# Sixteen places for the weight spreads of an expert loop, own sum banks for its second token tile, and later reads

## What is computed

```
q = h @ wq                                   # 8 heads, two halves of 128
sc = einsum(q, subkeys)                      # 128 keys for each half
vals, ids = top_k(sc, 16)                    # per half
top, pos = top_k(all 16 x 16 sums, 16)       # 16 experts per head, 128 per token
idx = the expert numbers (of 16384), g = softmax(top)
for the 128 experts k of a token:
    a   = dot(peer_u[idx_k], h)              # a row of 1024
    wgt = g_k * gelu(a)
    out += wgt * peer_v[idx_k]               # a row of 1024
x = x + gate2 * out
```

## Time and profile before

| what | us |
|---|---|
| median of 3 runs (1365.33 to 1369.11) | 1368.21 |
| the profiled execution, its own time | 1367.95 |
| its span, first to last instruction | 1366.2 |
| busy: PE / DVE / POOL / ACT | 1222.2 / 866.4 / 521.8 / 425.4 |
| expert loop, first gather to last sum | 174.7 to 870.4 |

### The profile page before, as it was taken

How to read it: one execution, slowest core, us unless ns; L and a number is a source line. 1 busy time by engine, 2 the same in 40 slices (tenths; PEclk the granted TensorE clock), 3 DMA queues, 4 the chain that set the end, 5 groups by cost and what they waited for, 6 DMA issues and landing times.

```text
span 1366.2 us, 14256 instructions
## 1 busy us (share of the span) xinstructions
PE 1222.2 (89%) x4539; PEld 642.2 (47%) x4539; DVE 866.4 (63%) x1726; ACT 425.4 (31%) x1126; POOL 521.8 (38%) x578
## 2 busy tenths in 40 slices
PE   7999979999877877877898777899999999999997
PEld 2676545565322222323443222564444445999443
DVE  2446478575575766777667578568997443677335
ACT  2212244333443343443434434322115111222000
POOL 1000057665777776777777777001111000000000
PEclk9999999999999999999999999999999999999999
DMA  9797599999999999999999999363333344354440
GB/s 346 294 328 278 171 334 398 406 406 404 405 409 410 409 409 409 392 409 409 409 409 407 408 406 404 145 246 123 124 123 124 107 157 166 140 183 146 169 181 31
DMA packets 130794, 397.32 MB, mean 291 GB/s; under 512 B 10380, under 2 KB 11788, under 8 KB 130463
## 3 DMA queue, kind: packets, MB, share of 16 engines
q0 software_dynamic: 74448, 271.09, 50.3%
q1 hardware_dynamic: 54404, 120.14, 24.4%
q10 hardware_dynamic: 1868, 5.18, 1.0%
HBM read 395.32 MB, written 1.05 MB: 290 GB/s over the span
## 4 chain that ended last, share of the span: by engine, by line
PE 46%; DMA 22%; POOL 12%; DVE 10%; issue 5%; DVEq 3%; ACT 1%; POOLq 0%; ACTq 0%
PE psum L673 18%; DMA gathered<-in_peer_u_dram,expert_idx 16%; PE psum L1270 6%; PE psum L1309 6%; POOL gathered L582 6%; POOL gathered L596 6%; PE psum L985 6%; DMA gathered<-in_peer_v_dram,expert_idx 3%; DVE work L1771 3%; DMA weight_ring<-in_w_in_dram 2%; DVE gathered L2116 2%; DVE work L2405 2%; PE psum L781 2%; PE psum L700 1%; PE psum L755 1%
## 5 line engine op out<-in xcount | busy, mean ns | idle before, releaser
L985 PE MATMUL psum<-gathered,modr 128*128 128x512 f32 x1024 | 500.1, 618 | 115.1 <-DMA gathered<-in_peer_v_dram,expert_idx 96.9
L2116 DVE CUSTOM_DVE_ANT_0 gathered<-gathered,psum 128x1024 f32<-128x1024 f32 x256 | 312.2, 1220 | 181.4 <-DMA gathered<-in_peer_u_dram,expert_idx 180.0
L985 PEld LDWEIGHTS psum<-gathered,modr 128*128 128x128 f32 x1024 | 180.0, 192 | 412.9 <-DMA gathered<-in_peer_v_dram,expert_idx 245.9
L582 POOL DMA_INDIRECT gathered<-in_peer_u_dram,expert_idx x256 | 249.0, 972 | 265.1 <-DVE expert_idx L1779 167.4
L596 POOL DMA_INDIRECT gathered<-in_peer_v_dram,expert_idx x256 | 243.8, 952 | 92.5 <-issue 70.8
L673 PE MATMUL psum<-weight_ring,featT 128*128 128x512 f32 x384 | 172.2, 603 | 1.7 <-ACT featT L1361 1.7
L1524 ACT ACTIVATE gel<-dots 128x1 f32<-128x1 f32 x256 | 51.6, 201 | 285.6 <-DVEq L2118 285.4
L1771 DVE TENSOR_TENSOR work<-work 128x1088 f32<-128x1088 f32 (+4 forms) x107 | 99.9, 951 | 26.8 <-ACT work L1624 18.7
L673 PEld LDWEIGHTS psum<-weight_ring,featT 128*128 128x128 f32 x384 | 71.7, 191 | 92.2 <-issue 90.0
L673 PE MATMUL psum<-featT,weight_ring 128*128 128x128 f32 (+2 forms) x768 | 107.6, 296 | 3.6 <-ACT featT L1361 1.5
L673 PEld LDWEIGHTS psum<-featT,weight_ring 128*128 128x128 f32 x768 | 100.6, 191 | 19.2 <-issue 11.5
(11 more groups left out here) (365 smaller groups left out, 1370.0 us busy)
## 6 DMA issues: line engine op xcount, KB each, us to landing
weight_ring<-in_w_in_dram SPq DMA_DIRECT2D x13, 2048.0 KB, 9.1
weight_ring<-in_ada_w_dram SPq DMA_DIRECT2D x10, 2048.0 KB, 17.5
weight_ring<-in_w_up_dram SPq DMA_DIRECT2D x8, 2048.0 KB, 8.3
weight_ring<-in_w_down_dram SPq DMA_DIRECT2D x8, 2048.0 KB, 7.7
weight_ring<-in_peer_wq_dram SPq DMA_DIRECT2D x3, 2048.0 KB, 12.7
gathered<-in_ada_w_dram SPq DMA_DIRECT2D x2, 2048.0 KB, 14.6
gathered<-in_w_in_dram SPq DMA_DIRECT2D x2, 2048.0 KB, 13.4
gathered<-in_peer_u_dram,expert_idx POOLq DMA_INDIRECT x256, 11.0
```

The lines of the kernel that those rows point to most:

```text
L582: pool.indirect_dma_start(u_rows[:, slot, :], None, T["peer_u"], bass.IndirectOffsetOnAxis(ap=expert_idx[:, r % 2, k:k + 1], axis=0),).the ...
L985: mm = pe.matmul(psum[:, SUM_BANK + half, :], diag[:, e % 8, :], v_rows[:, slot, 512 * half:512 * (half + 1)], start=(e % EXPERTS == 0), s ...
L2116: dve.tensor_tensor_reduce(u_rows[:, slot, :], u_rows[:, slot, :], h2_rows[t], 1.0, 0.0, ALU.mult, ALU.add, dots[:, col:col + 1])
```

## The change

- **Places for spreads.** `diag` gets eight more places, in `vec`. `rotate` gives each of the 256 experts the least recently used place: eight up to expert 75 of tile 0, sixteen from expert 76 on. ACT waits for the expert that last had the place.
- **Sum banks.** `sum_bank` gives tile 0 banks 2 and 3 and tile 1 banks 6 and 7. `u0` and `q20` move to banks 2 and 3. PE's wait for `sum_read` moves from tile 1's first expert to the first `u0` product, expert 58. DVE reads tile 0's sums after expert 14.
- **Reads and their places.** ACT reads tile 0's second-block products (and `meta`, `h0`, ln0) six experts behind PE. `u0` and `q20` stand every fourth expert, from 58 and from 76; ln0 every fourth from 84 in tile 0.
- **DVE.** A dot waits for the spread 15 experts back. The gate part of a route piece becomes one of its own, 23 pieces, the last three at 27 to 29 of a step; in tile 0's first 12 experts each piece has a drain before it. `first_tile_input` goes to experts 21 to 26 and 40 to 42, the s5 arguments to 80 to 84, the table pieces to 122 to 127.
- Sums are signalled by pairs before and after; ACT now counts the pairs of the place's last user.

```diff
@@ -70,20 +70,20 @@
...
 H2_BANK = (6, 0)
-SUM_BANK = 2
 TURN_H2 = 6
+ND, MORE_DIAG = 8, 76
...
 LATE_LOAD = 5
-META_AT, META_READ = 33, 36
-H0_AT, H0_READ = (37, 40), (40, 43)
-U0_AT = {47: 0, 50: 1, 53: 2, 56: 3}
-Q20_AT = {62: 0, 65: 1, 68: 2, 71: 3}
-COLUMN_LAG = 3
-LN0_AT = {96: 0, 98: 1, 100: 2, 102: 3}
+READ_LAG = 6
+META_AT = 43
+H0_AT = (50, 51)
+U0_AT = {58: 0, 62: 1, 66: 2, 70: 3}
+Q20_AT = {76: 0, 80: 1, 84: 2, 88: 3}
+LN0_AT = {84: 0, 88: 1, 92: 2, 96: 3}
@@ -181,7 +181,7 @@
...
 for _i in range(4):
-    NARROW.update({("u0", _i): (6, 7), ("q20", _i): (6, 7), ("k20", _i): (0, 1)})
+    NARROW.update({("u0", _i): (2, 3), ("q20", _i): (2, 3), ("k20", _i): (0, 1)})
@@ -193,6 +193,29 @@
...
         _uses[_bank] += 1
+def rotate(first, more):
+    at, before, turn = [], [], []
+    last, uses = {}, {}
+    for e in range(TT * EXPERTS):
+        places = first + [k for lo, hi, ks in more if lo <= e < hi for k in ks]
+        k = min(places, key=lambda k: (last.get(k, -1), k))
+        at.append(k)
+        before.append(last.get(k))
+        turn.append(uses.get(k, 0))
+        last[k], uses[k] = e, uses.get(k, 0) + 1
+    return at, before, turn
+D_AT, D_BEFORE, _ = rotate(list(range(ND)), [(MORE_DIAG, TT * EXPERTS, range(ND, 2 * ND))])
+def sum_bank(e):
+    return 2 if e < EXPERTS else 6
@@ -316,9 +339,14 @@
...
         rows = G[:, :].rearrange("p (s n) -> p s n", s=NU + NV)
-        u_rows, v_rows = rows[:, 0:NU, :], rows[:, NU:NU + NV, :]
+        u_rows = rows[:, 0:NU, :]
+        def v_row(e):
+            return rows[:, NU + e % NV, :]
         h2_rows = [psum[:, b:b + 2, :].rearrange("p b n -> p (b n)") for b in H2_BANK]
-        diag = modr[:, 0:D].rearrange("p (s n) -> p s n", s=8)
+        diag = [modr[:, P * i:P * (i + 1)] for i in range(ND)]
+        diag += [vec[:, 2 * D + P * i:2 * D + P * (i + 1)] for i in range(ND)]
@@ -594,7 +622,7 @@
...
                 pool.indirect_dma_start(
-                    v_rows[:, slot, :], None, T["peer_v"],
+                    v_row(e), None, T["peer_v"],
@@ -978,12 +1006,11 @@
...
-                slot = e % NV
-                pe.wait_ge(v_full[slot], 16 * (e // NV + 1))
+                pe.wait_ge(v_full[e % NV], 16 * (e // NV + 1))
...
                 for half in range(2):
-                    mm = pe.matmul(psum[:, SUM_BANK + half, :], diag[:, e % 8, :],
-                                   v_rows[:, slot, 512 * half:512 * (half + 1)],
+                    mm = pe.matmul(psum[:, sum_bank(e) + half, :], diag[D_AT[e]],
+                                   v_row(e)[:, 512 * half:512 * (half + 1)],
@@ -1029,7 +1056,6 @@
...
-            pe.wait_ge(flag("sum_read"), 1)
@@ -1038,6 +1064,7 @@
...
                 if e == min(U0_AT):
+                    pe.wait_ge(flag("sum_read"), 1)
@@ -1528,9 +1555,11 @@
...
                 act.drain()
-                if e >= 8:
-                    act.wait_ge(flag("pair_summed"), pairs(e - 7))
-                act.activation(diag[:, e % 8, :], ident[:, :], ACT.Copy,
+                if D_BEFORE[e] is not None:
+                    act.wait_ge(flag("pair_summed"), pairs(D_BEFORE[e] + 1))
+                elif D_AT[e] >= ND:
+                    group_wait(act, "ada", 11)
+                act.activation(diag[D_AT[e]], ident[:, :], ACT.Copy,
@@ -1567,10 +1596,11 @@
...
                     read_ada(ADA_AT[e - 3])
-                if e - 1 in LN0_AT:
-                    i = LN0_AT[e - 1]
+                if e - READ_LAG in LN0_AT:
+                    i = LN0_AT[e - READ_LAG]
                     read_turn(vec[:, 512 * i:512 * (i + 1)], turn_bank("ln0", i, 0), "ln0", i, 0)
-                if e == 70:
+                if e == 92:
+                    read_wait(act, "ada", 11)
@@ -1580,26 +1610,26 @@
...
                 weigh_expert(EXPERTS + e)
-                if e == 26:
+                if e == 29:
...
                     ln_root(0, "l0")
-                if e == META_READ:
+                if e == META_AT + READ_LAG:
                     to_features("meta", 0, 0, META)
-                if e in H0_READ:
-                    to_features("h0", 0, META, parts=(H0_READ.index(e),))
-                if e - COLUMN_LAG in U0_AT:
-                    read_columns("u", 0, U0_AT[e - COLUMN_LAG])
-                if e - COLUMN_LAG in Q20_AT:
-                    read_columns("q2", 0, Q20_AT[e - COLUMN_LAG])
+                if e - READ_LAG in H0_AT:
+                    to_features("h0", 0, META, parts=(H0_AT.index(e - READ_LAG),))
+                if e - READ_LAG in U0_AT:
+                    read_columns("u", 0, U0_AT[e - READ_LAG])
+                if e - READ_LAG in Q20_AT:
+                    read_columns("q2", 0, Q20_AT[e - READ_LAG])
...
                     softmax_exp(4 + e // ROUTE + 2)
-                if e == 76:
+                if e == 68:
...
                     act.activation(s5_dt[:, :], s5_dt[:, :], ACT.Exp).then_inc(flag("s5_dt_exp"), 1)
-                if e == 94:
+                if e == 88:
@@ -2097,15 +2127,18 @@
...
                         pick[:, 1, cols]).then_inc(flag("idx_ready"), 1)
+                elif i == 20:
...
                     dve.tensor_reduce(rsm[:, 2 + h0:2 + h1], top[:, hs, :], X, ALU.add)
-                elif i == 20:
+                elif i == 21:
                     dve.reciprocal(rsm[:, 2 + h0:2 + h1], rsm[:, 2 + h0:2 + h1])
-                elif i == 21:
+                elif i == 22:
...
-            ROUTE_PIECES, FIRST_NEXT = 22, 6
+            ROUTE_PIECES, FIRST_NEXT = 23, 6
+            PIECE_AT = {k: k for k in range(20)}
+            PIECE_AT.update({27: 20, 28: 21, 29: 22})
@@ -2113,19 +2146,21 @@
...
                 dve.wait_ge(u_full[slot], 16 * (e // NU + 1))
+                if e >= TOPK:
+                    dve.wait_ge(flag("diag_full"), e - TOPK + 1)
...
                 r, k = e // ROUTE, e % ROUTE
-                if e < ROUTE_PIECES // 2:
-                    route_piece(1, 2 * e)
-                    dve.drain()
-                    route_piece(1, 2 * e + 1)
+                if e < (ROUTE_PIECES + 1) // 2:
+                    for i in range(2 * e, min(2 * e + 2, ROUTE_PIECES)):
+                        dve.drain()
+                        route_piece(1, i)
...
                     route_piece(2, e - FIRST_NEXT)
-                if r and r + 1 < STEPS and k < ROUTE_PIECES:
-                    route_piece(r + 2, k)
+                if r and r + 1 < STEPS and k in PIECE_AT:
+                    route_piece(r + 2, PIECE_AT[k])
@@ -2156,7 +2191,8 @@
...
                     sl = slice(512 * half, 512 * (half + 1))
-                    last = tt(peer_out[:, sl], psum[:, SUM_BANK + half, :], gate2[:, sl], ALU.mult)
+                    last = tt(peer_out[:, sl], psum[:, sum_bank(EXPERTS * t) + half, :], gate2[:, sl],
+                              ALU.mult)
@@ -2342,24 +2378,26 @@
...
                     add_mod(10)
-                if e - 10 in ADA_AT:
-                    add_mod(ADA_AT[e - 10])
+                if e - 24 in ADA_AT:
+                    add_mod(ADA_AT[e - 24])
...
                 dot_expert(EXPERTS + e)
-                if e == 1:
+                if e == 14:
                     read_sum(0)
-                if ROUTE_PIECES <= e < ROUTE_PIECES + 9:
-                    first_tile_input(e - ROUTE_PIECES)
-                if 88 <= e < 93:
-                    s5_argument_piece(e - 88)
+                if 21 <= e < 27:
+                    first_tile_input(e - 21)
+                if 40 <= e < 43:
+                    first_tile_input(e - 34)
+                if 80 <= e < 85:
+                    s5_argument_piece(e - 80)
...
                     s5_matrix_piece(e - 116)
-                if 120 <= e < 126:
-                    table_piece(0, e - 120)
+                if 122 <= e < 128:
+                    table_piece(0, e - 122)
```

## The result

The changed kernel takes **1370.6 us** (median of 22 runs, 1365.3 to 1372.1), the kernel before 1367.4 us in the same session (22 runs, 1364.7 to 1369.2). The ratio is 1.0020 with a 95% interval of 1.0012 to 1.0027: slower by 1.6 to 3.7 us. The forecast was 1.5 us faster. The time lies in the range, and the difference is within the 0.3% that I had called no change, but its sign is wrong, and the interval leaves no doubt of the sign. The profiled execution of the changed kernel took 1370.25 us, its span is 1368.5; this is the execution that all rows of after come from.

A forecast was written before the change was run, and what follows sets the result against it. The prediction took the expert loop to be bound by the bytes its DMA engines move. Step 1's -1.5 us, with every other term at 0, took 1368.21 to 1366.7 us; the range was 1363.5 to 1371.1 us.

The forecast's parts named there:

- Step 3: Expert loop: DVE's new wait before a dot for the spread 15 experts back, long done by then; 0 us.
- step 2: Expert loop: sixteen places for spreads from expert 76 of tile 0 on, as eight never held ACT up; 0 us.
- Step 1: Turn of the tiles: new sum banks remove PE's wait for DVE and bring back missing bytes; -1.5 us, bounds 0 and -3.5.
- Step 6: Tile 1, experts 14, 41, 42, 80 to 83: DVE work falls together, rows under way cover it; 0, bound +3.2 us.
- step 4: Expert loop: reads six experts behind and products every four experts remove ACT waits, but bytes cover the gain; 0 us.
- step 5: Expert loop: route pieces with added drains in tile 0's first experts and later gate pieces; 0, with +0.8 us kept as bound.
- Step 7: Tail: moved table products and PE's wait for the k2 weights after the loop; 0, bounds 0 and -0.8 us.
- DVE as the bound of the u gathers: Rival, expert loop: DVE's lateness of steps 5 and 6 goes through one for one, +4.0 less 1.5, 1370.7 us; chance 0.12.

The follow-up runs named there:

- tables_late: The kernel before with only the six table pieces moved, to experts 122 to 127 instead of 120 to 125; 1367.63 us, ratio 1.0007.
- route_again: The kernel before with only the routing in 23 pieces, gate pieces at 27 to 29 and the added drains, on a fast chip; ratio 0.9998.
- schedule_again: The kernel before with only the new times of transposes, products and their later reads, on a fast chip; ratio 1.0002.
- places_again: The kernel before with only the sixteen spread places and DVE's added wait before each dot, on a fast chip; 3.1 us slower.
- banks_again: The kernel before with only the new sum banks and the moved wait and read of tile 0's sums, on a fast chip; ratio 0.9999.
- tables_back: The changed kernel with only the table pieces put back to experts 120 to 125; 1369.49 us, ratio 1.0014 to the kernel before.
- no_wait_again: The changed kernel without DVE's added wait, sixteen places kept, on a slower chip; ratio 1.0002 to the kernel before.

## Why the prediction was wrong

**Step 3, the added wait at 0, is the step that failed.** The timed runs show that steps 2 and 3 together, both put at 0, cost 3.1 us; the traces point to step 3. It argued that the spread 15 back is long done, and that holds: ACT's waits for DVE stayed at 2.5 us at the longest, no trace shows DVE waiting for ACT, and the added waits last 21 ns each, but for the one that shares its instruction with a wait for a row. But a wait that never holds is still an instruction. I priced its holding and not its presence: 239 instructions are 1.9 loads of 128. "The change moves no byte" is wrong by two packets of 8 KB; that is nothing in a sum of bytes, and yet the loop is 1.7 us longer in the mean. The other part of the 3.1 us, behind the loop, stays open.

**Step 1 was right that the waits go and wrong in what they are worth.** PE's 3.01 us and POOL's 2.15 us went. The 1.47 us of missing bytes did not come back, for two reasons. The first is that some executions never lose them. tables_late has the same turn as before, with the same wait of PE. PE's timeline of tables_late:

```profile
540.04 7.24 PE L985 MATMUL psum<-gathered,modr 128*128 128x512 f32 x16 [3.00 <-DVE modr L1771]
547.87 1.98 PE L985 MATMUL psum<-gathered,modr 128*128 128x512 f32 x4 [0.58 <-DMA gathered<-in_peer_v_dram,expert_idx]
```

Its windows there, and then the window of before from 540 us:

```profile
545.00:550.00 5.00, 4.26 (x10) 1.35 (x8) 4.60 (x15) 1.80 (x6) 3.74 (x4) 1.00 1.03 408
550.00:555.00 5.00, 3.06 (x7) 1.27 (x8) 3.19 (x10) 1.80 (x6) 3.66 (x4) 1.00 1.03 410
```
```profile
540.00:545.00 5.00, 4.36 (x5) 1.85 (x6) 4.76 (x17) 1.38 (x5) 3.06 (x4) 0.50 1.03 410
```

PE catches up at 1.8 us per expert and the DMA engines never run dry. In the profiled execution of before the granted clock stood at 0.50, the lower level, just as PE was to catch up, so it needed 2.26 us per expert, and the v places came free late. Of the five fast-chip traces with the old turn, before and route_again have that fall and tables_late, schedule_again and places_again don't; route_again lost 0.4 us of bytes by it. I had the row with the clock of 0.83 and didn't ask whether it is part of the kernel or of this one execution. The second reason is that even there the hole is no lost time. From dot 128 to dot 145 before takes 44.1 us, banks_again, without the wait at the turn, 44.3, and their whole loops are 685.24 and 685.19 us. The landings show why: at dot 138 the first part is 4.3 us ahead of the last in before and 6.7 us in tables_late, while the last part comes 5.0 and 5.1 us after that of dot 136, which is the usual time for two. So the missing bytes are, as I read it, those of DMA engines that were ahead.

**Step 6, "rows under way cover it", failed in the rows and hardly in the time.** The windows at experts 41 and 42 fell to 295 GB/s, 1.8 us of bytes by the same reckoning as in step 1, where the bound was 3.2. The pile-up was of the size told, but the case of 2.22 us that I compared it with was a single wait; here two came behind each other, and a gather was stretched to 1.53 us beside the normalisation. The rule of the Trainium skill on the port pair (SBUF — State Buffer, section SBUF: two separate sides), weighed in the prediction, agrees with that row. Yet undoing all three moves gave 1369.5 for 1369.5 of tables_back, and from dot 145 to dot 180 after takes 91.1 us, as places_again does without the pile-up: the time does not follow this hole.

**Steps 2, 4 and 5 at 0**: schedule 1.0002 and route pieces 0.9998 bear out 4 and 5; step 2 was never timed apart from the wait on a fast chip. **Step 7 at 0**: tables_late bears out the move itself (1.0007 with 1 in its interval); PE's 0.76 us wait for k2 vanished in after only because PE came later.

**The rivals.** The one that ended slower, DVE as the bound of the u gathers at 1370.7, hit the time by luck and not the cause: it rested on steps 5 and 6. The range reached the measured time only because it had to reach this rival. The case that came true wasn't among them.

## What to carry to other kernels

In a loop whose DMA engines are full, count instructions per turn of the loop, waits that never hold among them: compare the packets of the instruction queues of both pages, and look for a period in the starts of the loop's instruction that waits for a transfer. A transfer is done when its last part lands, so a mean rate over all DMA engines can fall without costing time, and one engine can be late without a sign in the mean. A hole read from one profiled execution is lost time only if other executions have it too; where the granted clock is down beside it, ask for a second trace before the hole enters the sum. A part of a change that should cost nothing is worth one run alone.

## What the runs showed of the hardware

- Instructions are loaded during the execution, in packets of 8 KB for VectorE, ACT, POOL and SP together (37 packets for 4790 instructions in before, 39 for 5046 in after) and of 16 KB for PE (37 for 9466).
- On the fast chips, one dot in about 128 VectorE instructions starts 0.94 us late, with rows streaming at 407 to 409 GB/s. It is the last of the 16 parts of its row that is late, while the middle one keeps its 2.5 to 2.7 us.
- A fall of the granted clock cost 1.7 or 3.4 us of full clock in the ten fast traces. The falls at about 190, 320 and 1030 us stand in all ten, those at 378 or 539 us in six, at 789 us in two, and those at 870 and 1070 us vary. The 33 runs of the kernel before in the first session (1363.9 to 1368.9 us) nearly order by their mean granted clock: 1368.0 at 0.990, 1366.7 at 0.992, 1364.5 at 0.995. The 35 runs of the third don't: 1366.8 at 0.990, 1366.2 at 0.992, 1367.3 at 0.993.
- The same kernel takes 1367 us on one chip and 1431 to 1442 us on another, with a mean granted clock of 0.966 for 0.992 in the second session. The loop of no_wait_again, the changed kernel without the wait, moves 363 GB/s on such a chip, for 407 of before on a fast one.
